# Writing queries and keys to the scratch in memory: 12 transfers of 64 partitions a pair in place of 24 of 32

## The reference, cut to what matters

```
x <- LN(alpha*x + 0.5*SwiGLU_a(x))
x <- LN(alpha*x + Mixer(x))
x <- LN(alpha*x + 0.5*SwiGLU_b(x))
```

```
# forgetting heads
s = einsum('bqhd,bkhd->bhqk', q_blk, k) * scale
s = s + c_q - c_k ; s = where(k_pos <= q_pos, s, NEG_INF)
# differential heads, for each of two maps m
s = einsum('bqhmd,bkhmd->bhmqk', q_blk, k) * scale
s = s - slope * (q_pos - k_pos) ; masked alike
```

## Time and profile before

| what | value |
|---|---|
| median of 3 runs | 1900.06 us (1899.64 to 1900.58) |
| profiled execution | 1899.35 us, its span 1897.6 us |
| TensorE busy | 1867.6 us (98%) |
| VectorE busy | 1411.4 us (74%) |
| ScalarE busy | 741.0 us (39%) |
| GpSimd busy | 217.0 us (11%) |
| DMA moved | 215.95 MB in 43747 packets, 8756 of them under 512 B |
| transfers of `put` | 192 from `hl`, 48 from `wloD`, 64 KB each, 1.7 us from issue to landing |

### The profile page before, as it was taken

One profiled execution on the slowest core, in us unless ns is written; L12 is line 12 of the kernel. 1 busy time (PEld: TensorE's weight loads), 2 busy tenths in 40 slices (PEclk: granted clock), 3 DMA queues, 4 the chain that ended last, 5 costly groups with the idle time before them and its releaser, 6 DMA issues.

```text
span 1897.6 us, 25000 instructions
## 1 busy us (share of the span) xinstructions
PE 1867.6 (98%) x9121; PEld 1572.7 (83%) x9121; DVE 1411.4 (74%) x2059; ACT 741.0 (39%) x1114; POOL 217.0 (11%) x247
## 2 busy tenths in 40 slices
PE   7999999999999999999999999999999999999998
PEld 6888888889888888888888888888888888888886
DVE  7877877952676878787897777777536688777777
ACT  5332333434554423333253242423455543424243
POOL 2000000153323000000100000003343220000001
PEclk9999999999999999999999999999999999999999
DMA  5222223236742222222313222223557323222221
GB/s 215 100 111 88 111 88 133 91 119 179 207 115 90 111 88 111 88 111 88 133 69 131 89 111 88 111 111 107 153 156 210 89 83 115 111 88 111 88 111 45
DMA packets 43747, 215.95 MB, mean 114 GB/s; under 512 B 8756, under 2 KB 11252, under 8 KB 20008
## 3 DMA queue, kind: packets, MB, share of 16 engines
q1 hardware_dynamic: 40808, 199.30, 29.7%
q0 software_dynamic: 2880, 15.90, 3.6%
HBM read 197.23 MB, written 17.93 MB: 113 GB/s over the span
## 4 chain that ended last, share of the span: by engine, by line
PE 90%; DVE 5%; issue 2%; ACT 1%; DMA 1%; POOL 1%; SPq 0%; ACTq 0%; DVEq 0%; POOLq 0%
PE psum L1011 80%; PE psum L1216 5%; PE psum L1313 2%; DVE res L1540 1%; PE psum L1303 1%; PE psum L1042 1%; PE psum L1291 1%; DVE st L1557 1%; DVE negm L1898 1%; DVE xlo L1496 0%; DMA gbc<-in_gb_col 0%; PE psum L1415 0%; PE psum L1242 0%; POOL rstd L609 0%; ACT psum L919 0%
## 5 line engine op out<-in xcount | busy, mean ns | idle before, releaser
L1011 PE MATMUL psum<-xhi,whiA 128*128 128x512 f32 (+1 forms) x768 | 287.4, 374 | 4.9 <-DVE xlo L1496 4.9
L1011 PE MATMUL psum<-xlo,whiA 128*128 128x512 f32 (+1 forms) x768 | 285.9, 372 | 0.0
L1011 PE MATMUL psum<-xhi,wloA 128*128 128x512 f32 (+1 forms) x768 | 285.8, 372 | 0.0
L1011 PE MATMUL psum<-xhi,whiB 128*128 128x512 f32 x704 | 273.9, 389 | 0.0
L1011 PE MATMUL psum<-xlo,whiB 128*128 128x512 f32 x704 | 273.9, 389 | 0.0
L1011 PE MATMUL psum<-xhi,wloB 128*128 128x512 f32 x704 | 273.9, 389 | 0.0
L1011 PE MATMUL psum<-whiD,hl 128*128 128x512 f32 x768 | 264.0, 390 | 2.0 <-DVE wloD L1473 2.0
L799 ACT ACTIVATE s<-psum 128x512 f32<-128x512 f32 x40 | 23.9, 598 | 540.7 <-PE psum L1011 540.6
L1651 DVE SCALAR_TENSOR_TENSOR res<-psum,res 128x1024 f32<-128x1024 f32 x120 | 146.7, 1222 | 82.1 <-PE psum L1011 82.1
L1651 DVE SCALAR_TENSOR_TENSOR nat<-psum,nat 128x1024 f32<-128x1024 f32 x144 | 175.8, 1221 | 26.3 <-PE psum L1011 26.3
L1011 PEld LDWEIGHTS psum<-xhi,whiA 128*128 128x128 f32 x768 | 145.4, 189 | 32.4 <-DVE xlo L1496 6.0
(11 more groups left out here) (230 smaller groups left out, 3520.5 us busy)
## 6 DMA issues: line engine op xcount, KB each, us to landing
rawA<-in_a_w SPq DMA_DIRECT2D x62, 1024.0 KB, 6.3
rawB<-in_b_w SPq DMA_DIRECT2D x54, 1024.0 KB, 4.8
rawD<-in_d_w SPq DMA_DIRECT2D x46, 1024.0 KB, 4.7
stacks<-hl SPq DMA_DIRECT2D x192, 64.0 KB, 1.7
whiD<-stacks POOLq DMA_DIRECT2D x10, 768.0 KB, 6.4
wloD<-stacks POOLq DMA_DIRECT2D x10, 768.0 KB, 5.9
gbr<-in_gb_row SPq DMA_DIRECT2D x6, 1024.0 KB, 8.4
stacks<-wloD SPq DMA_DIRECT2D x48, 64.0 KB, 1.7
```

Source lines behind the costliest of these rows:

```text
L1011: ins = t_.matmul(out_, a_, b_, start=(start and k == 1), stop=(stop and k == n), skip_group_check=check)
```

## The change

```
                 def put(b, tile, order, put_ok):
 
-                    for s in range(4):
+                    for h in range(2):
                         for j, part in enumerate(order):
-                            sp.dma_start(stacks[b, s // 2, j * ROWS:(j + 1) * ROWS, tile + s % 2, :],
-                                         part[s * ROWS:(s + 1) * ROWS, :].bitcast(F32)).then_inc(put_ok, 16)
+                            sp.dma_start(stacks[b, h, j * ROWS:(j + 1) * ROWS, tile:tile + 2, :].rearrange("r q n -> q r n"),
+                                         part[h * HD:(h + 1) * HD, :].bitcast(F32)).then_inc(put_ok, 16)
```

Each transfer now takes the 64 partitions of one head, and its destination is written as 2 tiles of 32 rows. There are 6 for a query and 6 for a key. The three places that wait for the counts change with it, `16 * 12 * n` to `16 * 6 * n`:

```
-                    pool.wait_ge(q_put, 16 * 12 * n)
-                    pool.wait_ge(k_put, 16 * 12 * n)
+                    pool.wait_ge(q_put, 16 * 6 * n)
+                    pool.wait_ge(k_put, 16 * 6 * n)
...
-                        act.wait_ge(q_put, 16 * 12 * (l * BODIES + b))
+                        act.wait_ge(q_put, 16 * 6 * (l * BODIES + b))
...
-                        act.wait_ge(k_put, 16 * 12 * (l * BODIES + b))
+                        act.wait_ge(k_put, 16 * 6 * (l * BODIES + b))
```

## The result

The changed kernel takes 2056.22 us (median of 6 runs, 2054.96 to 2058.16), the kernel before 1900.16 us beside it: 1.0825 times as long, with a 95% interval of 1.0813 to 1.0838. The forecast was 2062 us in a range of 2015 to 2185. The profiled execution took 2056.12 us, its span is 2054.4 us.

What follows compares the result with a forecast made beforehand. TensorE, busy 1867.6 of 1897.6 us, was taken to bound the kernel. Two layers at 81 us add 162 to the profiled 1899.35, giving 2061.4; the median stands 0.7 higher, so 2062, range 2015 to 2185.

Steps and rivals of the forecast that it cites:

- Two slices a transfer: Each put transfer is cut along its destination's leading 2: 128 KB on 2 engines instead of 16; 5156 small packets.
- The price of a row: A 2 KB row takes 0.088 us on its engine; at 0.077 the time is 2028, at 0.128 it is 2185.
- overlapping packets: Rival: packets of one engine overlap, effective row price 0.044, 13 us lost a layer, 1927 us; chance 4%.
- The queue from pair 1 on: Two engines never empty from 466.1 to 622 us: 135 us of sets, 10 of fills, 11 of stack loads, 156 together.
- Pair 0: First fill of rawA stands behind twelve transfers, landing about 441 us; TensorE loses 7.6 us a layer before L1011.
- The signs: Expected in the new profile: TensorE before L1291 in bodies 1 to 4 and L1011 once, ScalarE at L713 for rawA.
- ScalarE's stop in the bodies adds nothing: ScalarE's wait for the rawA fill in bodies 0 to 2 adds 0, since the same queue feeds both.
- theory A: Experiments' theory: destination's slowest dimension sets the slices, always on the same engines, whose queue sets how long bodies 0-3 last.
- the other theory's range: Four slices: no change, 1900 to 1904; with fill moved, late fill is the loss, 1900-1910 or 1900-1912. Eight: SP's issue, 1915-1927.
- The clock: TensorE's granted clock falls during its waits; charged 0, body 4 at most 20 us a layer, 40 us kept in range.
- The sum: Body 4 begins 81 us late in each layer with nothing else late behind it: 162 us in all.
- SP's issue: Twelve issues of 0.65 us a pair instead of 24 of 0.49 save SP 4 us, worth 0 since hidden.

Runs made afterwards that it cites:

- two_slices_24: Kernel before, still 24 transfers of 64 KB a pair, but stack rows reordered so each destination is 2 groups of 16 rows: 2052.24 us, 1.0806.
- woven_64: Changed kernel's 12 transfers of 64 partitions, weight columns reordered so each destination leads with 32 rows of 2 tiles: 1901.02 us, 1.0013.
- woven_128: Both heads in one transfer, 6 a pair of 128 partitions and 256 KB, destination 32 rows of 4 tiles; against the kernel before 1901.09 us, 1.001.
- fill_ahead: Changed kernel with the fill of the next weights moved between put_query and put_key in SP's queue: 2063.66 us, 1.0865.
- fill_own_queue: Changed kernel with four rawA fills a layer issued by GpSimd, with a completion count of their own: 2061.67 us, 1.0852.

## Why the prediction was right, step by step

- *Two slices a transfer.* Right, to the packet (5156), and two_slices_24 and woven_64 show that it is the destination's leading dimension and nothing else of the merge. (The source led with 32, 64 or 128 partitions in every kernel, so what its side does to the cut was not tested.) The Trainium skill's rule (DMA: Bandwidth & Descriptors, "Why a DMA increments its semaphore by 16 and not by 1") holds at 2, 4, 8 and 32: 2, 4, 8 and 16 completions. Its advice to merge small transfers ("Rules for kernel authors") brought nothing by itself in woven_64 and woven_128: the transfers, of 64 KB, were hidden.
- *The price of a row.* I took 0.088 us; in a full queue it is 0.0805. Eight sets of six are 8 x 192 x 0.0805 = 124 us and not 135, 11 us a layer less. My bounds were also summed wrongly: they carry the other prices through the eight sets but keep pair 0's 7.6 us, which hang on the same price. At 0.128 pair 0 alone adds 384 x 0.040 = 15.4 us a layer and the sum is 2216, not 2185; at 0.077 it is 2020, not 2028; and with overlapping packets it comes near 1910, not 1927.
- *The start of the queue.* I had no term for it. Two engines that start from empty are slow at first: the first 8 us of pair 1, then the next 8, in the changed kernel:

```profile
DMA packets 128, 0.26 MB, mean 32 GB/s; under 512 B 3, under 2 KB 3, under 8 KB 128
```
```profile
DMA packets 204, 0.43 MB, mean 54 GB/s; under 512 B 6, under 2 KB 6, under 8 KB 201
```

  That is 125 rows (468.2 to 476.2 us) and then 195 (476.2 to 484.2), 70 fewer, worth 70 x 0.0805 / 2 = 2.8 us. At pair 0 it is 124 rows from 403.7 to 411.7 us and then 198, worth 3.0 us.
- *The queue from pair 1 on.* It ran from 468.2 us to about 618, when the last keys had been written (SP had issued the fill behind them by 610.4, and POOL loaded the stack at 619.29); that is 150 us where I had 156. With 10 us of fills and 11 of stack loads the rows would make 145, so some 5 us were lost that I had not charged. The slow start is 2.8 of them. It began 2 us later than I had it. Body 4 began 77.0 us late; I had 81.
- *Pair 0.* 7.4 us before L1011, forecast 7.6, and ScalarE started on the fill at 441.10, forecast 441. That is luck. Twelve transfers at the real price take 384 x 0.0805 = 30.9 us and not 33.8, and the start that I left out adds 3.0: 33.9.
- *The signs.* I had TensorE standing before L1291 at bodies 1 to 4. It stood there only at body 4; in bodies 0 to 2 it stood at L1313, for ScalarE. The length of the bodies came out, the place where TensorE waits did not.
- *ScalarE's stop in the bodies adds nothing.* It was the boldest step, since the profile after shows it as the largest wait. fill_ahead and fill_own_queue bear it out: the stop went, and the time rose by 5 to 7 us. It holds for the full queue only; with four or eight slices what stands behind what matters, and in all four kernels there the time lay outside what theory A gave, in three of them outside the other theory's range as well.
- *The clock.* I charged 0 and kept 40 us. Windows of the changed kernel, 430 to 450 us and body 4 (us, busy of each engine, granted clock, DMA share, GB/s):

```profile
430.00:450.00 20.00, 12.59 (x57) 11.99 (x57) 2.29 (x1) 5.51 (x10) 2.25 (x4) 0.75 0.66 195
```
```profile
625.60:648.00 22.40, 21.58 (x125) 19.15 (x126) 11.73 (x37) 9.92 (x26) 2.74 (x3) 0.87 0.09 20
```

  After its long waits TensorE works at the lower level (1.2 GHz) for a while (from 508 to 511 us, after the wait of 16.2 us, it is busy throughout and granted 0.50), and its busy time in the whole kernel is 1889.5 - 1867.6 = 21.9 us longer. Only what falls outside the full queue counts: body 0 began 10.2 us late (471.92 for 461.72) of which 7.4 were waited, so about 3, and behind body 4 about 2.4 (the fill of `rawB` at 658.81 us for 579.34, 79.5 us late, against 77.0 at its start). That is some 5 us a layer, where I had none.
- *The sum.* 79.5 us in the first layer and 156.8 in all, against 81 and 162. Part of that nearness is luck: the row taken too dear (11 us a layer) cancels against the slow start (3), the clock (5) and 2 us that stay open.
- *SP's issue.* I had 4 us a pair saved. SP lost time instead, held by the full queue. I charge nothing more for it, since what it issued next stood behind the same work; no run tests this by itself.

## What to carry to other kernels

Before merging transfers, write down the slowest dimension of what each is to write (here only the destination's was varied): merged in the wrong order, half as many transfers ran on an eighth of the engines. Choose the layout so that the rows lead (here by weaving two halves in the weights' columns), and ask first whether anyone waits for the transfers, since otherwise even a quarter of them gains nothing. And when the same busy DMA engines feed two consumers, the wait that the profile shows as the largest may not be the one to lift; move one transfer to its own queue and see whether the wait only changes its name.

## What the runs showed of the hardware

- SP's issue takes longer when the engines it writes to are behind: 0.43 us a transfer before, 2.45 us median and up to 6.8 us in the changed kernel, and 2.4 us for a fill.
- The issue itself depends on the form: 0.43 us (median) for 32 rows in one dimension, 0.58 us in 4 groups, 0.62 us in 8, 0.60 us for 64 rows to 32 x 2.
- Two engines that start from empty move 124 or 125 rows in their first 8 us and 195 to 198 in the next, which costs about 3 us at each start (the changed kernel, pairs 0 and 1).
- Two-kilobyte rows on two engines with nothing beside them go at 0.0805 us each once the queue is full, 25.4 GB/s an engine, near the 26.6 GB/s of the busiest stretch with 8 KB rows; the time that their packets take, gaps left out, is 0.131 x 16 x 6 / 149 = 0.084 us a row, where with all 16 engines writing it was 0.128.
- What stays open: why both woven kernels are 0.1% above the one before (intervals that just exclude 1), why the first rows of a queue go slower, and the 2 us a layer that are left between the rows' sum and the queue's length.
